# A decoder step on one core: index keys stored in operand layout, sample attention spread over the projections

## The chip, the cores and the metric

One core of a Trainium2 chip runs the whole layer. The engines are named as in the profile: PE (matmul; PEld its weight load), DVE (vector), ACT (scalar), POOL, and SP, which only issues DMAs here. The metric is the device time of one launch in microseconds (us). Three timed runs of the kernel before gave 902.44, 902.24 and 901.87 us, a median of 902.24.

## The reference

One layer for a prompt of 512 new tokens and for 8 sample sequences of 4 new tokens each with 2048 cached positions. The parts that matter here:

```python
hn = _rmsnorm(x, g_pre_mix)
xl, gate, q, k, v, qi, ki, wi = _split_proj(hn @ w_in)      # and rotary on q, k, qi, ki
lru, hT, new_buf = _rglru(xl, ...)                          # conv taps, block gates, linear recurrence
att = attend(q, k, v, qi, ki, wi)
mix = concat(lru * gelu(gate), att) @ w_out                 # then norm, residual, squared-ReLU MLP

# a sample sequence: keys of 16 cached pages + 4 new ones
ki_past = cache_kidx[page_table].reshape(DB, PAST_LEN, IDX_DIM)
sc = einsum(relu(einsum(qi, ki_all) * IDX_DIM**-0.5), wi) * IDX_HEADS**-0.5
_, idx = top_k(where(kpos <= qpos, sc, -inf), 256)
# softmax over the 256 chosen keys (gathered from cache_k and cache_v), 8 heads of 64
```

The prompt has the same indexer and attention among its own 512 positions, with 128 chosen keys. The kernel does not gather the chosen keys: it scores all of them and adds a mask of 0 or -2^100.

## The kernel before, in words

All activations are stored transposed, channels on partitions and the 544 tokens (512 + 32) on the free axis, in two halves of 272. Each engine has its own straight program; the order on an engine is the order in which the code is written, and semaphores with counts tie the engines together. PE's program is the spine:

1. The input norm, then the projections of the index queries (QI, 4 tiles of 128 channels), of index key and head weights (KW), and the first tile of Q. A tile is 2 halves of 8 matmuls (`product`, L1229, `tile_product`, L1239); POOL applies the rotary (`rope`, L436) to what ACT copies out of PSUM (`rotary_tile`, L538).
2. The prompt's indexer (L1280 to L1290): scores on PE, ReLU on ACT (L584), weighting on DVE (L977). DVE then picks the prompt's top 128 (L987 to L993) and after it the sample's top 256 (L1008 on), one after the other.
3. The sample's indexer (L1293 to L1330), in two groups `g` of four sequences. POOL gathers the cached index keys by page table, 16 keys of 64 numbers to a partition (`gather`, L423, four gathers to a group into `kidx_in_sb`). PE transposes them (L1304), ACT copies the result to `kidxT` (L591), PE multiplies with the index queries (L1318), ACT applies the ReLU (L601), and PE sums the heads (L1325). Tile 1 of Q stands between the groups, tiles 2 and 3 after them.
4. K, XL (recurrent branch), GATE and V projections (L1372 to L1387). After every tile `unit_end` (L1361) does two *key steps* (`key_scores`, L1335): a step is one page of keys of four sequences, four DMAs of 256 KB issued by SP (`stream`, L358) into one of three slots of `kv`. 32 steps make the sample's scores `S`. The first needs `qbd`, which ACT builds (L617) from the rotated Q. The same `unit_end` also carries the recurrence of the four channel tiles: taps on ACT (`lru_taps`), sums on POOL (L463), gates on PE and ACT (`lru_gate`, L1358; `lru_gates`, L642), decay, root, and a scan on DVE (L1006) that frees the buffers for the next tile.
5. Scores of the new keys (L1394); ten mask products (L1408), each followed by a DVE add and maximum on `S` (L1068); two exponentials of 128 x 2080 on ACT (L720).
6. The prompt's attention, 32 units of one head and one query block (L1481): scores L1451, masked maximum on DVE L1081, exponential on ACT L736, transposes L1463, values L1476. In the same loop stand the ten transposes of the sample's probabilities (L1421) and one *value step* to a unit (`value_products`, L1426): a page of values of four sequences, streamed by SP through five slots, three of `kv` and two in the weight ring `wring`.
7. The sample's result is scaled (L1108), transposed (L1498) and copied, and the output projection (L1517) and the MLP follow, as long as everything before.

Weights come in blocks of 2 MB in the two halves of `wring`, loaded by SP or ACT (`load_block`, L555) when the block before in that half has been used.

## Time and profile before

| what | value |
|---|---|
| timed runs | 901.87 to 902.44 us, median 902.24 |
| the profiled execution | 901.47 us, its span 899.6 us |
| PE busy | 821.6 us, 91% of the span |
| DVE, ACT, POOL busy | 389.3, 348.5, 149.5 us |
| sample's indexer (stage 3) | from 79.4 us to the next Q tile at 113.0 |
| first key step | 139.1 us |
| masks (stage 5) | from 306.6 us |
| prompt attention with the value steps | 312.6 to 410.5 us |
| output projection starts | 414.55 us |
| DMA traffic | 133.21 MB, 148 GB/s on average; 383 GB/s from 350 to 410.5 us |

Times of a row are from the start of the span; the profiled execution is 1.87 us longer than its span and 0.77 us under the median. In a timeline row stand start, duration, engine, line, operation, output and inputs, count of records, and in brackets how long the engine had been idle and what ended that. A matmul in 32-bit floats leaves two records, so a tile of 16 matmuls shows as x32.

### The profile page before, as it was taken

The numbers are of one execution on the slowest core, as the hardware profiler recorded it, in microseconds if no ns is written. First come the engines' busy times: TensorE is split into PE (matmuls) and PEld (weight loads), VectorE is DVE, ScalarE is ACT, GpSimd is POOL, SyncE is SP. The second block draws the span as 40 slices with busy tenths as digits, with TensorE's granted clock in tenths as the row PEclk, the third lists the DMA queues.
The fourth block names the chain that finished last, engine by engine and source line by source line (L and its number), as shares of the span: only waits on it lengthen the run. The fifth ranks groups of instructions, "written<-read, shape, count | busy, mean of one in ns | idle before, by whom it ended". The sixth has DMA issues, their size and how long they took to land.

```text
span 899.6 us, 16220 instructions
## 1 busy us (share of the span) xinstructions
PE 821.6 (91%) x6089; PEld 673.0 (75%) x6089; DVE 389.3 (43%) x780; ACT 348.5 (39%) x744; POOL 149.5 (17%) x153
## 2 busy tenths in 40 slices
PE   5987799989999897988997999999999999999990
PEld 3863477777765442335886899999999999999990
DVE  6219999994000342430178544332212433433327
ACT  3556465355555462431253434322222433322120
POOL 0631064433233500000000111100000111100000
PEclk9999999999999987997998999999999999999996
DMA  8420416777758869992011222222222222222202
GB/s 343 161 94 28 159 72 206 253 258 241 247 191 300 281 233 391 387 387 89 1 48 47 71 79 85 93 95 80 84 93 94 71 93 93 70 95 94 93 24 99
DMA packets 52180, 133.21 MB, mean 148 GB/s; under 512 B 6113, under 2 KB 6626, under 8 KB 50850
## 3 DMA queue, kind: packets, MB, share of 16 engines
q1 hardware_dynamic: 49442, 113.08, 36.3%
q10 hardware_dynamic: 864, 10.58, 3.3%
q0 software_dynamic: 1824, 8.86, 2.6%
q8 instruction: 33, 0.54, 0.2%
q14 instruction: 17, 0.14, 0.0%
HBM read 127.84 MB, written 4.67 MB: 147 GB/s over the span
## 4 chain that ended last, share of the span: by engine, by line
PE 74%; DVE 7%; DMA 6%; SPq 5%; ACT 4%; issue 3%; POOL 1%; DVEq 0%; ACTq 0%
PE bank L1529 42%; PE bank L1235 20%; SPq L365 4%; PE bank L1346 3%; PE bank L1384 3%; DMA arena<-in_ck 3%; DMA wring<-in_cv 2%; DVE scp L977 1%; PE bank L1358 1%; ACT lx L634 1%; PE bank L1318 1%; PE bank L1304 1%; DVE lx L913 1%; DMA arena<-in_cv 1%; PE bank L1434 1%
## 5 line engine op out<-in xcount | busy, mean ns | idle before, releaser
L1235 PE MATMUL bank<-regR,wring 128*128 128x272 f32 x640 | 152.8, 399 | 7.5 <-DVE regR L924 4.4
L1235 PEld LDWEIGHTS bank<-regR,wring 128*128 128x128 f32 x640 | 122.0, 192 | 35.3 <-issue 5.3
L1164 DVE TENSOR_TENSOR h_lo<-lx,h_hi 128x544 f32 (+1 forms) x32 | 35.9, 1121 | 111.0 <-ACT h_hi L827 110.7
L1529 PE MATMUL bank<-h_lo,w_hi_odd 128*128 128x272 f32 x256 | 73.9, 289 | 0.0
L1529 PE MATMUL bank<-h_hi,w_hi_even 128*128 128x272 f32 x256 | 73.8, 288 | 0.0
L1529 PE MATMUL bank<-h_lo,w_hi_even 128*128 128x272 f32 x256 | 73.7, 288 | 0.0
L1529 PE MATMUL bank<-h_hi,w_hi_odd 128*128 128x272 f32 x256 | 73.7, 288 | 0.0
L1529 PE MATMUL bank<-h_hi,w_lo_odd 128*128 128x272 f32 x256 | 73.6, 287 | 0.0
L1529 PE MATMUL bank<-h_hi,w_lo_even 128*128 128x272 f32 x256 | 73.5, 287 | 0.0
L506 POOL TENSOR_TENSOR lx<-lx 128x544 f32<-128x544 f32 x30 | 32.8, 1093 | 244.6 <-ACT lx L822 244.6
L1529 PE MATMUL bank<-hn_lo,w_hi_odd 128*128 128x272 f32 x240 | 69.3, 289 | 0.0
L1529 PE MATMUL bank<-hn_hi,w_hi_even 128*128 128x272 f32 x240 | 69.3, 289 | 0.0
L1529 PE MATMUL bank<-hn_lo,w_hi_even 128*128 128x272 f32 x240 | 69.1, 288 | 0.0
L1529 PE MATMUL bank<-hn_hi,w_hi_odd 128*128 128x272 f32 x240 | 69.1, 288 | 0.0
L1529 PE MATMUL bank<-hn_hi,w_lo_odd 128*128 128x272 f32 x240 | 69.0, 287 | 0.0
L1529 PE MATMUL bank<-hn_hi,w_lo_even 128*128 128x272 f32 x240 | 68.9, 287 | 0.0
L1116 DVE TENSOR_TENSOR w_lo_even<-wring,w_hi_even 128x1024 fp32r<-128x1024 f32 x32 | 39.2, 1225 | 66.4 <-ACT w_hi_even L788 66.4
L822 ACT ACTIVATE lx<-bank 128x272 f32<-128x272 f32 x60 | 23.9, 398 | 113.7 <-PE bank L1529 113.7
L1235 PE MATMUL bank<-regM,wring 128*128 128x272 f32 x256 | 60.8, 400 | 2.0 <-ACT regM L763 2.0
L1235 PEld LDWEIGHTS bank<-regM,wring 128*128 128x128 f32 x256 | 49.6, 194 | 12.8 <-ACT regM L763 2.4
L1116 DVE TENSOR_TENSOR w_lo_odd<-wring,w_hi_odd 128x1024 fp32r<-128x1024 f32 x32 | 39.0, 1220 | 44.2 <-ACT w_hi_odd L788 43.9
L788 ACT CAST w_hi_even<-wring 128x1024 fp32r<-128x1024 f32 x32 | 33.6, 1049 | 62.5 <-PE bank L1529 62.5
(259 smaller groups left out, 1683.7 us busy)
## 6 DMA issues: line engine op xcount, KB each, us to landing
arena<-in_ck SPq DMA_DIRECT2D x128, 256.0 KB, 3.9
wring<-in_w_mlp SPq DMA_DIRECT2D x64, 512.0 KB, 3.4
arena<-in_cv SPq DMA_DIRECT2D x80, 256.0 KB, 5.7
wring<-in_cv SPq DMA_DIRECT2D x48, 256.0 KB, 6.1
wring<-in_w_in ACTq DMA_DIRECT2D x4, 2048.0 KB, 8.5
wring<-in_w_in SPq DMA_DIRECT2D x2, 2048.0 KB, 13.1
regX<-in_xT SPq DMA_DIRECT2D x4, 544.0 KB, 5.5
regX<-in_xT POOLq DMA_DIRECT2D x1, 2176.0 KB, 11.3
```

Source lines behind the costliest of these rows:

```text
L365: eng.dma_start(slot[:, b4, :], table[bass.ds(page[b4], 1), :, :].rearrange("a p c -> p (a c)")).then_inc(landed, 16)
L506: nc.gpsimd.tensor_tensor(square_t[:, s, :], relu_t[:, s, :], relu_t[:, s, :], ALU.mult).then_inc(h_sq, 1)
L634: nc.scalar.activation(out[:, 0:SEQ], prompt, ACT.Identity, bias=bias, scale=w)
L788: nc.scalar.copy(w_hi[parity][:, :], w_raw[:, parity, :]).then_inc(w_hi_rd, 1)
L822: nc.scalar.activation(relu_t[:, parity, hf * HALF:(hf + 1) * HALF], bank[(2 * parity + hf) % 4][:, 0:HALF], ACT.Relu).then_inc(h_ev, 1)
L913: ins = vec.reciprocal(rstd[:, c], rstd[:, c])
L1116: vec.tensor_tensor(w_lo[parity][:, :], w_raw[:, parity, :], w_hi[parity][:, :].bitcast(F32), ALU.subtract).then_inc(w_lo_rd, 1)
L1164: vec.tensor_tensor(h_lo[:, at], square_t[:, parity, :], h_hi[:, at].bitcast(F32), ALU.subtract).then_inc(h_lo_rd, 1)
L1235: ins = pe.matmul(bank[e % 4][0:parts, 0:HALF], lhs(k), rhs[:, k, hf * HALF:(hf + 1) * HALF], start=(k == 0), stop=(k == KT - 1))
L1346: ins = pe.matmul(bank[4 + s % 2][32 * b4:32 * b4 + 32, 0:P], qbd[:, 4 * (s // NPG) + b4, m, :], kv[:, slot, b4, m * P:(m + 1) * P], start ...
L1384: ins = pe.matmul(bank[e % 4][0:n, :], hnT[:, k, j * P:j * P + n], w[:, k, :], start=(k == 0), stop=(k == KT - 1))
L1529: ins = pe.matmul(out, lhs[w][:, k * P:(k + 1) * P], rhs(k), start=(first and k == 0 and i == 0), stop=(last and k == KT - 1 and i == 2))
```

## The change

Four things are changed together, and the diff below is cut to them.

- **Index keys.** The host stores each page as 64 x 128 (channel by key), so PE needs no transposes. A page now lands in `kidxT[g]` directly. For group 0, SP issues 64 small DMAs (32 KB each, before the key stream); for group 1, POOL issues 32 gathers of 128 rows of 512 bytes instead of four of 128 rows of 4 KB, placed between its rotary tiles. ACT copies Q's first tile out between the two groups.
- **Key steps.** One stands in the middle and one at the end of each *half* tile of K and XL, so all 32 are done two projections earlier.
- **Sample attention.** New scores, masks, exponentials, transposes and the first 21 value steps move into GATE and V; the other eleven stand at every third unit of the prompt's attention. V's 32 sample rows are projected first (`V_ORDER`). DVE does scans 1 to 3 after the masks.
- **Slots.** Values use three slots instead of five; both halves of the output weight are loaded by ACT.

```diff
-V_SLOTS = 5
+V_SLOTS = 3
+V_ORDER = (4, 0, 1, 2, 3)
+MID_VALUES = 21
...
@@ SP @@
+            def index_keys(j):
+                eng.load(page_regs, steps[0:1, j * 4:(j + 1) * 4])
+                rows, cols = HD * (j // 8), P * (j % 8)
+                for b4 in range(4):
+                    page = eng.snap(page_regs[b4], min_val=0, max_val=NPOOL - 1)
+                    eng.dma_start(kidxT[0][rows:rows + HD, b4, cols:cols + P],
+                                  ci_d[bass.ds(page, 1), :, :].rearrange("a d k -> (a d) k")).then_inc(kidx_in[0], 16)
             eng.wait_ge(steps_in, 16)
+            for j in range(NPG):
+                index_keys(j)
             keys(0, 2, None, 0)
-            keys(1, 0, kx_tr, 16)
-            keys(2, 1, kx_tr, 16)
+            keys(1, 0, kd_mm, 5)
+            keys(2, 1, kd_mm, 5)
...
@@ POOL @@
+            def index_keys(first, last):
+                for n in range(first, last):
+                    b4, j = n // 8, n % 8
+                    gather(kidxT[1][:, b4, j * P:(j + 1) * P], ci_rows, row_i[:, b4, j:j + 1], kidx_in[1])
+            eng.wait_ge(hn_rd, 2 * KT)
+            index_keys(0, 4)
             for t in range(CT):
                 rope(t, qiT[:, t, :])
+                index_keys(4 + 2 * t, 6 + 2 * t)
             rope(4, kiT[0:HD, :], HD)
-            eng.wait_ge(kx_tr, 8)
-            for b in range(4):
-                gather(kidx_in_sb[:, b, :], ci_rows, row_i[:, 4 + b:5 + b], kidx_in)
+            index_keys(12, 32)
...
@@ ACT @@
             for g in range(GRP):
-                for u in range(8):
-                    eng.wait_ge(kx_tr, 8 * g + u + 1)
...
+                if g == 1:
+                    rotary_tile(5, E_Q)
                 for d in range(5):
...
             for m in range(CT):
-                rotary_tile(9 + m, E_K + 2 * m)
-                sample_scores(2 * m)
-                sample_scores(2 * m + 1)
+                rotary_tile(9 + m, E_K + 2 * m, scores=4 * m)
...
+            gate_out(0, 0)
+            gate_out(0, 1)
+            recurrence(4)
+            gate_out(1, 0)
+            sample_transposed(0)
...
+            gate_out(2, 1)
+            sample_exponentials(1)
+            recurrence(6)
...
@@ DVE @@
-            for c in range(CT):
-                scan(c)
+            scan(0)
             for g in range(GRP):
...
+            for c in range(1, CT):
+                scan(c)
...
@@ PE @@
+            w = weights(2)
+            for m in range(CT):
+                for hf in range(2):
+                    s = 4 * m + 2 * hf
+                    half_product(E_K, hf, m, lambda: key_scores(s))
+                    key_scores(s + 1)
...
+            w = weights(4)
+            half_product(E_GATE, 0, 0, new_key_scores)
+            masks(0, 1)
+            half_product(E_GATE, 1, 0, lambda: masks(2, 3))
+            masks(4)
+            recurrence_gates(1)
...
+            for i, j in enumerate(V_ORDER):
...
+                    if k in (2, 5):
+                        value_products(6 + 3 * i + k // 3)
...
-            for u in range(KSTEPS + 5):
+            for u in range(ATT_UNITS + 5):
                 if u < ATT_UNITS and u % 2 == 0:
                     att_scores(u // 2)
-                if u < 10:
-                    sample_transposes(u)
...
-                if u >= 5:
-                    value_products(u - 5)
+                if u % 3 == 1 and MID_VALUES + u // 3 < KSTEPS:
+                    value_products(MID_VALUES + u // 3)
```

What this does to the order on the engines, at three places. First PE from the end of the prompt's indexer to the first key steps. Before, L1304 are the transposes, L1318 the index products, L1235 projections and L1346 key steps:

```order
L1289 MATMUL bank<-arena,regQ 128x512 x8
L1304 MATMUL bank<-ident,arena 128x128 x32
L1318 MATMUL bank<-regX,arena 32x512 x16
L1318 MATMUL bank<-arena 32x32 x4
L1235 MATMUL bank<-regR,wring 128x272 x16
L1304 MATMUL bank<-ident,arena 128x128 x32
L1318 MATMUL bank<-regX,arena 32x512 x16
L1318 MATMUL bank<-arena 32x32 x4
L1325 MATMUL bank<-regM,wm 32x512 x8
L1329 MATMUL bank<-regM,wm 32x32 x2
L1235 MATMUL bank<-regR,wring 128x272 x48
L1346 MATMUL bank<-arena,qbd 32x128 x32
```

And now, where L1344 are the index products, L1270 projections and L1371 key steps:

```order
L1326 MATMUL bank<-arena,regQ 128x512 x8
L1344 MATMUL bank<-arena 32x512 x16
L1344 MATMUL bank<-arena 32x32 x4
L1270 MATMUL bank<-regR,wring 128x272 x16
L1344 MATMUL bank<-regX,arena 32x512 x16
L1344 MATMUL bank<-arena 32x32 x4
L1350 MATMUL bank<-regM,wm 32x512 x8
L1354 MATMUL bank<-regM,wm 32x32 x2
L1270 MATMUL bank<-regR,wring 128x272 x36
L1371 MATMUL bank<-arena,qbd 32x128 x16
L1270 MATMUL bank<-regR,wring 128x272 x4
```

The two groups of 32 transposes are gone, and the first key step stands 36 matmuls after the head sums instead of 48: after half of the first half tile of K, not after its first tile.

The second place is the end of GATE and the start of V on PE. Before, L1358 are the recurrence's gates and L1384 the V projection:

```order
L1235 MATMUL bank<-regR,wring 128x272 x16
L1358 MATMUL bank<-lx,wgate 128x272 x2
L1346 MATMUL bank<-arena,qbd 32x128 x32
L1358 MATMUL bank<-lx,wgate 128x272 x2
L1384 MATMUL bank<-wring,regR 128x512 x8
L1346 MATMUL bank<-arena,qbd 32x128 x32
```

Now L1448 are transposes of the sample's probabilities, L1462 value steps, L1385 gates and L1522 the V projection:

```order
L1270 MATMUL bank<-regR,wring 128x272 x4
L1448 MATMUL bank<-ident,regX 128x128 x4
L1462 MATMUL bank<-arena,regQ 32x512 x4
L1270 MATMUL bank<-regR,wring 128x272 x4
L1385 MATMUL bank<-lx,wgate 128x272 x2
L1462 MATMUL bank<-arena,regQ 32x512 x4
L1385 MATMUL bank<-lx,wgate 128x272 x2
L1522 MATMUL bank<-wring,regR 32x512 x3
L1448 MATMUL bank<-ident,regX 128x128 x4
L1462 MATMUL bank<-arena,regQ 32x512 x4
```

A value step of four matmuls stands between the two pairs of gates where two key steps stood, and the projections are cut in pieces of two to four matmuls.

The third place is POOL after the rotary of the index key. Before:

```order
L440 TENSOR_TENSOR lx<-lx 64x544
L441 TENSOR_TENSOR lx<-lx 64x544
L442 TENSOR_TENSOR arena<-lx 64x544
L425 DMA arena<-in_ci,row_i 128x1024 x4
L440 TENSOR_TENSOR lx<-lx 128x544
```

And now:

```order
L452 TENSOR_TENSOR lx<-lx 64x544
L453 TENSOR_TENSOR lx<-lx 64x544
L454 TENSOR_TENSOR arena<-lx 64x544
L430 DMA regX<-in_ci,row_i 128x128 x20
L452 TENSOR_TENSOR lx<-lx 128x544
```

Twenty gathers instead of four stand in POOL's queue ahead of the rotary of Q.

## Rows read from the trace of the kernel before

**Rows 1.** The page, part 4: shares of the chain by engine.

```profile
PE 74%; DVE 7%; DMA 6%; SPq 5%; ACT 4%; issue 3%; POOL 1%; DVEq 0%; ACTq 0%
```

**Rows 2.** Stretches: length, busy (count) of PE, PEld, DVE, ACT, POOL, PEclk, DMA, GB/s.

```profile
313.00:350.00 37.00, 31.23 (x196) 14.18 (x194) 12.59 (x72) 17.49 (x57) 2.13 (x5) 0.74 0.79 291
350.00:410.50 60.50, 53.33 (x418) 19.52 (x414) 21.70 (x80) 20.68 (x51) 0.00 (x0) 0.95 1.04 383
```

**Rows 3.** Timeline of PE, the sample's indexer to the first key step.

```profile
79.44 6.18 PE L1304 MATMUL bank<-ident,arena 128*128 128x128 f32 x32 [2.11 <-ACT arena L584]
86.30 3.71 PE L1318 MATMUL bank<-regX,arena 128*32 128x512 f32 x32 [0.68 <-ACT regX L591]
...
97.50 1.04 PE L1304 MATMUL bank<-ident,arena 128*128 128x128 f32 x8
...
103.26 3.71 PE L1318 MATMUL bank<-regX,arena 128*32 128x512 f32 x32 [0.68 <-ACT regX L591]
...
113.00 23.95 PE L1235 MATMUL bank<-regR,wring 128*128 128x272 f32 x96 [3.18 <-ACT lx L550]
139.11 1.95 PE L1346 MATMUL bank<-arena,qbd 128*32 128x128 f32 x64 [2.16 <-issue]
```

**Rows 4.** The gathers' line L425 on POOL, and POOL's idle time before them.

```profile
L425 POOL DMA_INDIRECT arena<-in_ci,row_i x8: 933/948/1170, 24.4 to 89.7; - x8
...
  issue: 1.8, 6
```

**Rows 5.** Timeline of POOL: end of the index key's rotary, and two of Q's.

```profile
58.73 1.32 POOL L442 TENSOR_TENSOR arena<-lx 64x544 f32<-64x544 f32 x1
...
114.98 1.34 POOL L440 TENSOR_TENSOR lx<-lx 128x544 f32<-128x544 f32 x1 [24.39 <-ACT lx L550]
...
131.67 2.28 POOL L440 TENSOR_TENSOR lx<-lx 128x544 f32<-128x544 f32 x1 [3.27 <-ACT lx L550]
```

**Rows 6.** Timeline of ACT: last copy of Q, building qbd, a table load.

```profile
130.05 1.54 ACT L550 COPY lx<-bank 32x272 f32<-32x272 f32 x4
137.20 1.81 ACT L617 COPY qbd<-regQ 64x32 f32<-64x32 f32 x8 [5.61 <-POOL regQ L442]
...
223.47 1.28 ACT L642 ACT_TABLE_LOAD   x1
```

**Rows 7.** Timeline of PE: two key steps, a tile, a stalled key step.

```profile
148.53 1.95 PE L1346 MATMUL bank<-arena,qbd 128*32 128x128 f32 x64
150.41 7.60 PE L1235 MATMUL bank<-regR,wring 128*128 128x272 f32 x32
...
182.47 1.93 PE L1346 MATMUL bank<-arena,qbd 128*32 128x128 f32 x32 [4.62 <-DMA arena<-in_ck]
```

**Rows 8.** Timeline of SP: the key stream, and later two steps and two more.

```profile
14.35 265.72 SPq L365 DMA_DIRECT2D arena<-in_ck  x120
280.89 4.42 SPq L365 DMA_DIRECT2D wring<-in_cv  x8
285.97 4.42 SPq L365 DMA_DIRECT2D arena<-in_ck  x8
```

**Rows 9.** DMA issues, keys and weights: count, KB each, us to landing.

```profile
arena<-in_ck SPq DMA_DIRECT2D x128, 256.0 KB, 3.9
...
wring<-in_w_in ACTq DMA_DIRECT2D x4, 2048.0 KB, 8.5
```

**Rows 10.** The chain of waits in the XL stage: start, us, what.

```profile
170.22 12.21 DMA arena<-in_ck
```

**Rows 11.** Timeline of PE: first masks, first scores of the prompt's attention.

```profile
306.57 0.49 PE L1408 MATMUL bank<-smask,ind_r 32*128 32x512 f32 x2 [0.18 <-ACT arena L708]
...
312.60 0.80 PE L1451 MATMUL bank<-arena,regQ 64*128 64x128 f32 x4
```

**Rows 12.** Timeline of DVE: the sample's mask is done; the last scaling.

```profile
211.24 0.44 DVE L1056 TENSOR_SCALAR smask<-arena 128x544 fp32r<-128x544 f32 x1
...
410.64 0.75 DVE L1108 TENSOR_SCALAR lx<-bank,sstat 128x512 f32<-128x512 f32 x1 [8.40 <-PE bank L1438]
```

More of the change, by code:

```diff
@@ L229, in build @@
         w_in = [sem("w_in_even"), sem("w_in_odd")]
-        kidx_in = sem("kidx_in")
+        kidx_in = [sem(f"kidx_in{g}") for g in range(GRP)]
         kv_in = [sem(f"kv_in{i}") for i in range(3)]
@@ L381, in _ @@
                     keys(i * 3 + (3 + j), (j + 2) % 3, k_mm, i * 3 + (j + 1))
-            for s in range(3, V_SLOTS):
-                values(s, s, gemm_mm, E_V)
             for s in (30, 31):
@@ L545, in rotary_tile @@
                 for hf in range(2):
+                    if scores is not None:
+                        sample_scores(scores + 2 * hf)
                     src = gemm_out(e + hf)
@@ L553, in rotary_tile @@
                     last.then_inc(gemm_ev, 1)
+                    if scores is not None:
+                        sample_scores(scores + 2 * hf + 1)
             def load_block(n):
@@ new lines, in _, with gate_out @@
+            for m in range(CT):
+                s = 16 + 4 * m
+                sample_scores(s)
+                recurrent_half(m, 0)
+                sample_scores(s + 1)
+                sample_scores(s + 2)
+                recurrent_half(m, 1)
+                if m == 1:
+                    recurrence(m, lambda: sample_scores(s + 3))
+                else:
+                    sample_scores(s + 3)
+                    recurrence(m)
+            load_block(5)
+            def gate_out(m, hf):
+                src = gemm_out(E_GATE + 2 * m + hf)
+                nc.scalar.activation(mixT[:, m, hf * HALF:(hf + 1) * HALF], src[:, 0:HALF], ACT.Gelu_apprx_tanh).then_inc(gemm_ev, 1)
@@ new lines, in _ @@
+            w = weights(2)
+            for m in range(CT):
+                for hf in range(2):
+                    s = 4 * m + 2 * hf
+                    half_product(E_K, hf, m, lambda: key_scores(s))
+                    key_scores(s + 1)
+            w = weights(3)
+            for m in range(CT):
+                for hf in range(2):
+                    s = 16 + 4 * m + 2 * hf
+                    half_product(E_XL, hf, m, lambda: key_scores(s))
+                    if m == 1 and hf == 1:
+                        lru_gate(0, 0)
+                        lru_gate(0, 1)
+                    key_scores(s + 1)
+                if m == 1:
+                    lru_gate(0, 2)
+                    lru_gate(0, 3)
@@ new lines, in new_key_scores @@
+            def new_key_scores():
+                eng.wait_ge(rope_out, 13)
+                eng.wait_ge(k_ev, KSTEPS)
+                for g in range(GRP):
+                    for m in range(CT):
+                        for b4 in range(4):
+                            ins = pe.matmul(bank[4 + g][32 * b4:32 * b4 + 32, 0:NS], qbd[:, 4 * g + b4, m, :], kT[:, m, SEQ:NT],
+                                            start=(m == 0), stop=(m == CT - 1))
+                    ins.then_inc(kn_mm, 1)
@@ new lines, in sample_mask @@
+            def sample_mask(n):
+                g, c = n // 5, n % 5
+                cols = slice(c * 512, min((c + 1) * 512, NKEY))
+                if n == 0:
+                    eng.wait_ge(smask_rd, 1)
+                    eng.wait_ge(kn_ev, GRP)
+                elif n >= 2:
+                    eng.wait_ge(sm_ev, n - 1)
+                rows = slice(NS * min(c, 3), NS * min(c, 3) + NS)
+                taken = smask[rows, 0:CHUNK] if c < 4 else smask[rows, CHUNK:ROW]
+                pe.matmul(bank[4 + n % 2][:, 0:cols.stop - cols.start], ind_r[rows, g, :], taken, start=True, stop=True).then_inc(sm_mm, 1)
@@ new lines, in _ @@
+            transposes_and_values(6, 3)
+            half_product(E_GATE, 1, 3, lambda: transposes_and_values(7, 4))
+            recurrence_gates(2, lambda: value_products(5))
+            w = weights(5)
+            for i, j in enumerate(V_ORDER):
+                n = P if j < 4 else NS
+                e = E_V + i
+                slot_free(e)
+                for k in range(KT):
+                    ins = pe.matmul(bank[e % 4][0:n, :], hnT[:, k, j * P:j * P + n], w[:, k, :], start=(k == 0), stop=(k == KT - 1))
+                    if k == 2 and i < 2:
+                        sample_transposes(8 + i)
+                    if k in (2, 5):
+                        value_products(6 + 3 * i + k // 3)
+                ins.then_inc(gemm_mm, 1)
+                if i == 2:
+                    recurrence_gates(3, lambda: value_products(8 + 3 * i))
+                else:
+                    value_products(8 + 3 * i)
```

268 lines of the change are left out of this document (121 added, 147 removed).

## The prediction

> **What bounds the kernel now.** I read the chain of waits first, then the stretches, then PE's timeline stage by stage. The chain is 74% PE [rows 1], so a microsecond is won only where PE does work that can go, or stands still. From the first key step to the output projection the reader is to look at PE's busy time together with its granted clock: in the attention, 313 to 410.5 us, PE is busy 31.23 us at a mean clock of 0.74 and 53.33 us at 0.95 [rows 2]. At the full 2.4 GHz that is about 31.23 x 0.74 + 53.33 x 0.95 = 73.8 us of work in 97.5 us, so 23.7 us are lost there, while the DMA engines are full (share 1.04, 383 GB/s, rows 2): the 32 value steps are all streamed in this stage. Two other losses stand in PE's timeline: the transposes of the index keys, and the mask products. The MLP behind is untouched.
>
> **Index stage.** The transposes take 86.30 - 79.44 = 6.9 us and 103.26 - 97.50 = 5.8 us of PE's time, ACT's copies between them included, and tile 2 of Q then waits 3.18 us for ACT, which has not yet copied tile 0 out [rows 3]. The change copies that tile between the groups. So Q's tile 2 starts at 113.0 - 12.7 - 3.2 = 97.1 us and tile 3, with 7.5 us a tile (rows 7: 7.60 for x32, with an overlap), ends at 112.2. Then the gain is partly given back: half a half tile later, at 114.1, PE reaches the first key step, which needs qbd. Behind tile 3's end lie five copies on ACT (1.9 us; four take 1.54, rows 6), one rotary of three POOL operations of 1.34 (4.0 us, rows 5; not the 2.28 of the last one before, when DVE was in a different operation), and ACT's 1.81 (rows 6). That makes 120.1 us: PE waits 6.0 us with the rest of K queued behind. Before, the first key step ran at 139.11 with a whole tile of K done (7.5 us), now with a quarter (1.9). Lead: 139.1 - 120.1 - 5.6 = 13.4 us. After a 3.18 us wait the next three tiles took 23.95 instead of 22.6 us [rows 3]; I take the same 1.4 us off for the half clock after this wait. **11.9 us.**
>
> This needs the index keys in time. Group 0: 64 issues on SP. Two steps of four DMAs with their register loads start 5.08 us apart [rows 8], so 16 steps take 41 us from 14.35 us on [rows 8] and are 20 us early for 79.4; what they hold up, the first key loads, is wanted only at 120. Group 1: a gather costs POOL 0.95 us and 0.3 of idle [rows 4]. The twelve early ones fit into gaps in which POOL waits for ACT; the last twenty run from 60.05, the end of the index key's rotary [rows 5], to 85.1, and the dots of group 1 start at 79.4 + 3.8 + 7.5 = 90.7. The cover is 5.6 us, less landing; behind the gathers the rotary of Q is queued, for which nobody waits before 87. If the pitch were 1.55 us, the cover would be gone.
>
> The rows show gathers issued every 1.25 us without waiting for one another [rows 4]. The Trainium skill, "DMA: Bandwidth & Descriptors", section "Anatomy of one DMA — SWDGE (gpsimd) path", puts about 2 us of fixed cost on each such DMA, and its rules for kernel authors call transfers below 64 KB mostly overhead. If that cost were paid one after another, the last twenty would end at about 100 instead of 85 us; that is the first rival below.
>
> **Key steps.** The interval between key steps falls from 4.7 us to (7.5/2 + 2 x 0.95)/2 = 2.83 us [rows 7]. A step is four DMAs of 256 KB [rows 9], 1.05 MB, which is 2.74 us at 383 GB/s [rows 2], and 2.54 us of SP's time [rows 8]. Both are just below 2.83. From the release of a slot to its next use there are 3 x 2.83 - 0.95 = 7.5 us; the fourth DMA is issued 1.5 us after the release and lands 3.9 us later [rows 9], 5.4 us. So the K stage keeps up with 97% of the DMA rate; I take 1.5 us of jitter (0 to 14: half a microsecond on 28 steps). XL has the GATE weights (2048 KB, rows 9) and the stores of K (as much as half of that and a little) on top, 2.1 and 1.2 MB: 3.3 MB are 8.6 us at 383 GB/s, less 2.1 us of slack. Before, the same transfers made one step land after 12.21 us [rows 10] and PE wait 4.62 us [rows 7]. Net **-2 us** (1 to -8).
>
> The same page of the Trainium skill, section "Specifications", gives about 358 GB/s of HBM to a core, by which a step would take 2.93 us and the 29 streamed steps some 3 us more than I sum. The trace does not agree: 383 GB/s over 60 us [rows 2].
>
> **GATE and V.** Here PE only gets work that it did later: ten masks, ten transposes, 21 value steps. That shift is worth nothing by itself. What it removes: from the first mask to the first attention scores PE needed 6.0 us [rows 11] for ten products of some 0.25 us (0.49 for two): **+3.5 us**, the adds on DVE being hidden under GATE's products. The mask itself is ready at 211.2 [rows 12], by a chain on DVE that starts with the prompt's indexer and is not shortened; PE wants it at about 222 (120 + 43 of K + 54 of XL + 5), so it is not late. What it adds: ACT's gates need a table load of 1.28 us [rows 6], which two key steps (1.95 us) covered; now one step or none stands there. Some 0.9 us on each of four: **-3.5 us** (0 to -10; the two exponentials and eight copies also stand in ACT's queue between GATE's evictions). V runs three value steps in 7 + 3 us per tile, 3.4 us each, slower than the stream; the output weight's 2.1 MB in between costs **-1.5 us** (0 to -5).
>
> **Attention.** Eleven value steps instead of 32, 11.5 MB with 5.4 MB of x, V and weights, are 44 us of DMA in some 53 us, so the stream should no longer bound it. Bounds for the loss: 0, and the 23.7 us of today. I take 8, a third, for the start of the pipeline, the small first blocks where DVE and ACT set the pace, and the burst of other transfers: **+15.7 us** (0 to 23.7). At the end the first of the two scalings, 0.75 us [rows 12], is no longer hidden: **-0.8**.
>
> **Sum.** 11.9 - 1.5 - 2 + 3.5 - 3.5 - 1.5 + 15.7 - 0.8 = 21.8 us, from the profiled 901.47 to 879.7. The runs shown have their median 0.77 higher, so I say **880 us**.
>
> **Rivals.**
> - *Index keys late.* If the gathers cost 2 us each, the last lands near 102 us and PE waits 11 us at group 1: 891. For it: these gathers are eight times as many, and DVE is busy in the prompt's indexer meanwhile. Against: same 128 rows, same 0.95 us while DVE was picking [rows 4].
> - *The stream or PE's queue takes back more.* Half a microsecond per key step (14 us), or an attention that keeps most of its loss because DVE and ACT set its pace: 890 to 898. For it: 97% use with three slots, PE's program in order. Against: 3.9 us of landing in 7.5.
> - *Slower than before: the slot turn bounds the keys.* If under load every key step landed like the one of rows 10, a step would take (1.5 + 12.2 + 0.95)/3 = 4.9 us, 28 steps 57 us more, 937 us. It decides against the change from 21.8/28 = 0.78 us more per step on, a landing of 8.4 us. For it: one such landing is seen. Against: it shared the engines with two other transfers, and the stream of values held 383 GB/s [rows 2].
> - *Better.* Jitter, table loads and burst all hidden: 866 to 870.
> - *The work only moves*, and gives no time: within 0.2% (1.8 us, about what a measurement can tell).
>
> **How the numbers follow.** Forecast, 870 to 889: 0.52. Index keys late: 0.10. More taken back: 0.17. Better: 0.08. No change: 0.03. Slower: 0.10. Faster is 0.52 + 0.10 + 0.17 + 0.08 = 0.87, same 0.03, slower 0.10. The range 866 to 897 holds the forecast, the first two rivals nearly and most of the better case, some 0.8.
>
> **What would show it.** Right: no transposes between 79 and 97 us and the last head sum near 97; the first key step near 120 after a wait of about 6 us for ACT's qbd; key steps 2.8 us apart in K with waits on DMA only in XL; no stage of its own for the masks; an attention of 50 to 60 us with a clock near 1.0; the output projection starting near 393. Wrong: a wait for the index keys at 91 us, waits on DMA before most key steps in K, or an attention still over 75 us.

## The result, and the profile after

The changed kernel took **897.84 us** in the median (896.25 to 901.7, 11 runs) beside 903.44 us of the kernel before (901.87 to 907.61, 11 runs) on the same chip: a ratio of 0.9945, 95% interval 0.9929 to 0.9961. It is faster by 0.55% (5.6 us between the medians); 22 us were forecast. The time lies 0.84 us above the top of the range.

The profiled execution took 901.08 us (span 899.3), one of the slowest of the eleven. A second profile of the same kernel (e16 below, 898.61 us) is read beside it. Most of the miss lies between the first key step and the output projection, and there the two agree: 290.9 and 289.7 us.

The chain of waits, page part 4, shares of the span by engine and by line [rows 1]:

```profile
PE 84%; DVE 6%; DMA 4%; ACT 3%; issue 1%; POOL 0%; SPq 0%; ACTq 0%; DVEq 0%
PE bank L1617 42%; PE bank L1270 23%; PE bank L1522 4%; PE bank L1371 3%; PE bank L1462 3%; DMA arena<-in_cv 2%; DMA arena<-in_ck 1%; PE bank L1541 1%; PE bank L1553 1%; PE bank L1566 1%; PE bank L1256 1%; PE bank L1344 1%; DVE scp L1012 1%; DVE lx L948 1%; PE bank L1673 1%
```

PE holds 84% of it in place of 74%: the waits for others became PE's own work. The index stage, PE's timeline (start, us, line, tiles, count, idle before) [rows 3]:

```profile
82.25 3.82 PE L1344 MATMUL bank<-arena 128*32 128x512 f32 x40 [2.11 <-ACT arena L598]
86.00 7.60 PE L1270 MATMUL bank<-regR,wring 128*128 128x272 f32 x32
93.53 3.71 PE L1344 MATMUL bank<-regX,arena 128*32 128x512 f32 x32
...
98.04 1.92 PE L1350 MATMUL bank<-regM,wm 128*32 128x512 f32 x16 [0.68 <-ACT regM L610]
...
122.99 1.93 PE L1371 MATMUL bank<-arena,qbd 128*32 128x128 f32 x32 [6.20 <-issue]
```

The transposes are gone, the second group of index keys is not waited for at 93.53, and the first key step waits 6.20 us for qbd, as forecast (6.0). It stands at 123.0 and not at 120.1 because this execution ran its first 50 us at a mean clock of 0.93; in e16 the clock there was 1.00 and the step stood at 120.38. The last gather, POOL's timeline [rows 4]:

```profile
84.10 1.47 POOL L430 DMA_INDIRECT regX<-in_ci,row_i  x1 [0.30 <-issue]
...
88.38 0.94 POOL L430 DMA_INDIRECT regX<-in_ci,row_i  x1 [0.30 <-issue]
```

Key steps of K, and the stall in XL, PE's timeline [rows 7]:

```profile
131.63 1.08 PE L1371 MATMUL bank<-arena,qbd 128*32 128x128 f32 x32
132.64 2.10 PE L1270 MATMUL bank<-regR,wring 128*128 128x272 f32 x8
134.67 1.08 PE L1371 MATMUL bank<-arena,qbd 128*32 128x128 f32 x32
...
187.37 1.94 PE L1371 MATMUL bank<-arena,qbd 128*32 128x128 f32 x32 [7.00 <-DMA arena<-in_ck]
189.23 3.99 PE L1270 MATMUL bank<-regR,wring 128*128 128x272 f32 x8
```

The interval of two key steps is 134.67 - 131.63 = 3.04 us with no wait for data, where 2.83 was forecast. The start of the attention, PE, then DVE, then POOL:

```profile
340.54 0.49 PE L1541 MATMUL bank<-arena,regQ 64*128 64x128 f32 x4
346.27 1.08 PE L1553 MATMUL bank<-ident,arena 128*128 128x128 f32 x2 [5.24 <-DVE arena L1123]
...
350.79 1.93 PE L1462 MATMUL bank<-arena 128*32 128x512 f32 x8 [1.68 <-DMA arena<-in_cv]
...
359.62 1.93 PE L1462 MATMUL bank<-arena 128*32 128x512 f32 x8 [4.33 <-DMA arena<-in_cv]
```

```profile
340.85 5.36 DVE L1123 TENSOR_SCALAR arena<-arena,stat 128x128 f32<-128x128 f32 x1
346.53 0.29 DVE L1123 TENSOR_SCALAR arena<-arena,stat 128x128 f32<-128x128 f32 x1
```

```profile
340.53 1.35 POOL L502 TENSOR_TENSOR regM<-regM,arena 128x544 f32<-128x544 f32 x1
...
344.99 1.13 POOL L502 TENSOR_TENSOR regM<-regM,arena 128x544 f32<-128x544 f32 x1
```

The first normalisation on DVE takes 5.36 us, the next one 0.29, and it ends at 346.21 us, as POOL's four gate multiplications do (346.12). The stretches (columns as in [rows 2]): the K stage, then the attention.

```profile
139.00:172.00 33.00, 33.00 (x440) 24.47 (x439) 31.54 (x64) 13.13 (x38) 9.96 (x8) 1.00 1.00 344
...
339.00:347.00 8.00, 2.63 (x22) 1.07 (x18) 6.79 (x13) 2.54 (x8) 7.58 (x15) 0.77 0.98 343
347.00:372.00 25.00, 18.98 (x87) 7.10 (x91) 8.34 (x48) 7.77 (x32) 0.80 (x2) 0.53 0.88 335
372.00:410.00 38.00, 35.65 (x300) 17.64 (x292) 23.49 (x90) 22.18 (x59) 0.00 (x0) 1.00 0.38 123
```

Here the reader is to see two things. In K the DMA engines are full (share 1.00) at 344 GB/s, not at the 383 of the value stream before [rows 2]. And of 71 us of attention 2.63 x 0.77 + 18.98 x 0.53 + 35.65 = 47.7 us are work at 2.4 GHz: 23.3 us are lost, as many as before (23.7).

**Where the 17 us went.** PE's busy time times its granted clock, summed over slices of 1 us, is its work; the rest of the time is lost. K and XL count from the first key step to GATE's first product; the middle column runs on to the first scores of the attention, masks included; the attention ends at the transposes of the sample's result.

| length, work, lost | K, XL | GATE, V, masks | attention |
|---|---|---|---|
| before | 76.3, 70.0, 6.3 | 97.2, 90.9, 6.3 | 97.9, 74.0, 23.9 |
| after, e16 | 110.8, 97.0, 13.7 | 106.2, 103.4, 2.8 | 68.7, 48.7, 20.0 |

Over the three stages the work grew by 249.1 - 234.9 = 14.2 us, and the loss is 36.5 us in both. The sum of the prediction has 5.6 us more work here (three quarters of a K tile, now behind the first key step) and 8.5 us less loss (15.7 in the attention, 3.5 of masks, less 1.4, 1.5, 2, 3.5, 1.5 and 0.8). So **8.6 us are work that the sum did not have, and 8.5 us are losses that did not go**; together 17.1 us, the miss.

The work can be placed. In K and XL before has 70.0 us, to which the change adds the 5.6 and eight pairs of key steps of 1.9 us that stood in GATE and V: 90.8 us, where e16 has 97.0. That is 6.2 us more; the other two columns together have the other 2.4.

### The profile page after: what moved, and what is told of

It reads as the page before. It is cut to its first block, busy times and chain, and to the rows that moved or that the text cites. A ratio compares the mean times of both kernels' runs of the same rounds, so it can differ in the third digit from the quotient of the medians.

```text
span 899.3 us, 16317 instructions
## 1 busy us (share of the span) xinstructions
PE 824.6 (92%) x6025; PEld 664.1 (74%) x6025; DVE 387.2 (43%) x780; ACT 341.4 (38%) x730; POOL 173.9 (19%) x177
## 4 chain that ended last, share of the span: by engine, by line
PE 84%; DVE 6%; DMA 4%; ACT 3%; issue 1%; POOL 0%; SPq 0%; ACTq 0%; DVEq 0%
PE bank L1617 42%; PE bank L1270 23%; PE bank L1522 4%; PE bank L1371 3%; PE bank L1462 3%; DMA arena<-in_cv 2%; DMA arena<-in_ck 1%; PE bank L1541 1%; PE bank L1553 1%; PE bank L1566 1%; PE bank L1256 1%; PE bank L1344 1%; DVE scp L1012 1%; DVE lx L948 1%; PE bank L1673 1%
## 5 line engine op out<-in xcount | busy, mean ns | idle before, releaser
L1270 PE MATMUL bank<-regR,wring 128*128 128x272 f32 x640 | 166.2, 412 | 3.2 <-DVE regR L959 3.2
L1270 PEld LDWEIGHTS bank<-regR,wring 128*128 128x128 f32 x640 | 121.8, 196 | 38.8 <-issue 14.4
L857 ACT ACTIVATE lx<-bank 128x272 f32<-128x272 f32 x60 | 23.9, 398 | 113.7 <-PE bank L1617 113.7
L1270 PE MATMUL bank<-regM,wring 128*128 128x272 f32 x256 | 60.9, 401 | 2.3 <-ACT regM L798 2.3
L1270 PEld LDWEIGHTS bank<-regM,wring 128*128 128x128 f32 x256 | 49.6, 194 | 13.1 <-ACT regM L798 2.5
```

Of the source, the lines that this page charges most:

```text
L857: nc.scalar.activation(relu_t[:, parity, hf * HALF:(hf + 1) * HALF], bank[(2 * parity + hf) % 4][:, 0:HALF], ACT.Relu).then_inc(h_ev, 1)
L1270: ins = pe.matmul(bank[e % 4][0:parts, 0:HALF], lhs(k), rhs[:, k, hf * HALF:(hf + 1) * HALF], start=(k == 0), stop=(k == KT - 1))
```

## The experiments

Times are medians; ratios are to the kernel before, run beside on the same chip. Lengths are from PE's timelines, us: K and XL from the first key step to the first products with the new keys, then GATE and V, then the attention up to the output projection.

| run | us | ratio (95%) | first key step | K, XL | GATE, V | attention |
|---|---|---|---|---|---|---|
| after | 897.84 | 0.9945 (0.9929 to 0.9961) | 123.0 | 112.0 | 104.1 | 74.8 |
| e16 after again | 899.01 | 0.9945 (0.9924 to 0.9966) | 120.4 | 112.8 | 104.2 | 72.8 |
| e1 pairs | 900.79 | 0.997 (0.9955 to 0.9984) | 122.9 | 112.1 | 104.3 | 72.9 |
| e2 POOL first | 898.26 | 0.9948 (0.9929 to 0.9966) | 121.0 | 112.2 | 104.1 | 72.7 |
| e3 late reload, stores | 891.77 | 0.9868 (0.9841 to 0.9894) | 123.0 | 112.3 | 104.3 | 65.3 |
| e5 four slots | 896.08 | 0.992 (0.9895 to 0.9945) | 120.4 | 107.9 | 104.1 | 74.0 |
| e6 four slots, pairs | 893.68 | 0.99 (0.9878 to 0.9921) | 122.5 | 104.7 | 104.5 | 74.0 |
| e7 GATE weights later | 898.78 | 0.995 (0.9931 to 0.9968) | 121.6 | 110.4 | 104.5 | 74.1 |
| e8 = e6, e2, e3 | 884.93 | 0.9805 (0.9782 to 0.9828) | 120.7 | 105.0 | 104.6 | 66.4 |
| e10 first tile whole | 882.53 | 0.9764 (0.9744 to 0.9783) | 120.3 | 101.4 | 104.3 | 68.5 |
| e12 and GATE weights | 879.63 | 0.9742 (0.9719 to 0.9764) | 121.5 | 99.2 | 104.5 | 65.5 |
| e13 output block late | 891.91 | 0.9875 (0.986 to 0.9891) | 122.7 | 109.4 | 104.3 | 65.7 |
| e14 x late alone | 893.82 | 0.9893 (0.9877 to 0.9909) | 122.7 | 112.7 | 104.1 | 68.2 |
| e15 all late | 876.19 | 0.9704 (0.9686 to 0.9721) | 121.1 | 102.6 | 104.6 | 58.7 |

Three more have the order of the kernel before: e4 (896.75 us, 0.9924, 0.9903 to 0.9945), e11 (899.1 us, 0.9944, 0.9925 to 0.9962), e9 (916.44 us, 1.0169, 1.0139 to 1.02).

**e1, key steps in pairs.**

```diff
-                    half_product(E_K, hf, m, lambda: key_scores(s))
+                    half_product(E_K, hf, m, None)
+                    key_scores(s)
                     key_scores(s + 1)
```

> The two key steps of a half product of K and XL both stand behind it, so that no half of these 16 is cut in the middle; ACT's copies follow that order; all else is the changed kernel. Price-of-a-cut theory: before, a tile of K with one cut and two key steps took 9.42 us; after, with four cuts and four key steps, 12.16, so a cut costs (12.16 - 4 x 0.945 - 7.53)/3 = 0.28 us. Two cuts per tile go, on 8 tiles 16 x 0.28 = 4.5 us: about 893.3 us (ratio to the kernel before 0.9895), a tile of K at 11.6 us. Rival, each key step pays for its own wait wherever it stands: no change, 898 us (0.994), a tile still at 12.1. Rival, two key steps in a row run ahead of the stream: a wait on DMA in front of the second one, 898 us or more.

No faster than the change (0.997 beside 0.9945). The profile of e1 (PE) has the saving and what became of it:

```profile
151.12 1.08 PE L1370 MATMUL bank<-arena,qbd 128*32 128x128 f32 x32 [0.27 <-DMA arena<-in_ck]
152.13 3.94 PE L1269 MATMUL bank<-regR,wring 128*128 128x272 f32 x16
156.00 1.08 PE L1370 MATMUL bank<-arena,qbd 128*32 128x128 f32 x32
157.31 1.08 PE L1370 MATMUL bank<-arena,qbd 128*32 128x128 f32 x32 [0.23 <-DMA arena<-in_ck]
```

A whole half takes 156.00 - 152.13 = 3.87 us where two pieces took 2 x 2.03, but in K a wait for data of 0.23 to 1.50 us now stands before the second key step of five of the eight pairs: the stream cannot follow. The price of a cut is real and was hidden by the slots. The first theory had no such limit; the third expectation came true.

**e2, POOL's multiplications first.**

```diff
-            eng.wait_ge(gemm_ev, E_WO)
-            eng.dma_start(v_d[0:SEQ, :].rearrange("(j p) c -> p j c", p=P), v[:, 0:4, :]).then_inc(state_stored, 16)
-            eng.dma_start(v_d[SEQ:NT, :], v[0:NS, 4, :]).then_inc(state_stored, 16)
+            eng.wait_ge(gemm_ev, E_GATE + 2 * CT)
             for c in range(CT):
...
             eng.dma_start(lru_d, pack[:, :, :]).then_inc(state_stored, 16)
+            eng.wait_ge(gemm_ev, E_WO)
+            eng.dma_start(v_d[0:SEQ, :].rearrange("(j p) c -> p j c", p=P), v[:, 0:4, :]).then_inc(state_stored, 16)
+            eng.dma_start(v_d[SEQ:NT, :], v[0:NS, 4, :]).then_inc(state_stored, 16)
```

> POOL's four gate multiplications (with their small copies) stand ahead of the stores of V, so that they run right behind the last scan at some 333 to 339 us and are over when the attention's first normalisation on DVE comes; all else is the changed kernel. Theory that DVE's first normalisation of 5.36 us (0.29 for the others) is long because POOL multiplies at the same time: it takes 0.3 us, PE's wait of 5.24 us before the first transpose goes, 4 to 5 us faster, about 893.5 us (0.9895). Rival, the stream decides there: PE goes to its value step 22 sooner and waits that much longer for the data, which land when they land; 897 us (0.993).

DVE's first normalisation, and PE's next wait:

```profile
339.11 0.35 DVE L1124 TENSOR_SCALAR arena<-arena,stat 128x128 f32<-128x128 f32 x1
```

```profile
349.17 1.93 PE L1463 MATMUL bank<-arena 128*32 128x512 f32 x8 [7.73 <-DMA arena<-in_cv]
```

0.35 us in place of 5.36: the two engines did collide. But the time stays, since PE waits 7.73 us for value step 22 in place of 1.68. The rival had it right.

**e3, the reload of x and the stores of V behind value step 27.** The stores are taken from their place ahead of the multiplications.

```diff
             eng.wait_ge(st_tr, 10)
+            eng.wait_ge(v_mm, 28)
+            eng.dma_start(v_d[0:SEQ, :].rearrange("(j p) c -> p j c", p=P), v[:, 0:4, :]).then_inc(state_stored, 16)
+            eng.dma_start(v_d[SEQ:NT, :], v[0:NS, 4, :]).then_inc(state_stored, 16)
             eng.dma_start(regX[:, :], xT_d).then_inc(x_again, 16)
```

> The reload of x (2.2 MB) and the stores of V (1.1 MB) are issued behind value step 27 and not at the start of the attention; all else is the changed kernel. Theory that this burst keeps value steps 22 and 23 from landing: their waits of 1.68 and 4.33 us go, and with them the half clock up to 372 us; 6 us of waits, less what stays behind DVE's slow normalisation, and up to 3 us of clock: about 891 us (0.987; 888 to 895). Rival, the output weight's block (2.1 MB) or the three slots hold the stream anyway: 896 us (0.992). Rival, the late reload now stands in the way at the attention's end or of the residual: 900 us or more.

In time as the first theory has it: 0.9868 beside the change's 0.9945, some 7 us of 903. The attention is 7.4 to 9.4 us shorter in the profile than in the two of the change. The wait before step 23 is gone, but not the one before step 22:

```profile
348.58 1.93 PE L1463 MATMUL bank<-arena 128*32 128x512 f32 x8 [2.84 <-DMA arena<-in_cv]
```

POOL's multiplications still met DVE there, one at a time, and PE's wait for DVE falls to 0.89, 1.03 and 0.61 us in place of 5.24. So more than the two transfers changed here; e14, which keeps the 5.24, is the cleaner test:

```profile
341.25 1.01 DVE L1124 TENSOR_SCALAR arena<-arena,stat 128x128 f32<-128x128 f32 x1
342.58 1.04 DVE L1124 TENSOR_SCALAR arena<-arena,stat 128x128 f32<-128x128 f32 x1
```

**e4 and e11, the index keys' part alone, and with x's reload late.** The edit of e4 is the index part of the diff on the kernel before; e11 adds the wait for v_mm 28 ahead of the reload.

> The kernel before with the index keys' part of the change alone (layout, SP's and POOL's loads, no transposes, tile 0 of Q copied between the groups); the attention of the sample stands where it stood before. In the changed kernel this part brought the first key step from 139.1 to 123.0 us with a quarter tile of K done in place of a whole one: 10.5 us of lead. Theory that this lead is worth itself: 893 us (0.9885). Then the other part of the change, the spreading, loses 5 us net. Rival, the lead is lost at the attention, where the stream of values sets the pace but does not start earlier: no, since it starts with V's end, which moves too; still, if the mask of the top-k chain or the stream binds, 898 to 903 us (0.994 to 1.0), and the spreading gains 0 to 5 us.

> The index keys' part alone as in e4, and x's reload (2.2 MB) behind value step 27; the attention of the sample stands where it stood before. Theory that the late reload is worth as much without the spreading, since there the stream of values bounds the attention and gets rid of 2.2 MB at 386 GB/s, 5.6 us: 891 us (0.986). Then the spreading in itself gains nothing (e3 has 891.8). Rival, without the spreading the values do not come faster, or the reload now stands before the residual: 896 us (0.992).

The index part alone is as fast as the whole change (0.9924 and 0.9945, overlapping intervals), so the spreading as it stands gains nothing that was measured. The first key step of e4 is 17.3 us earlier, the first scores only 7.0 (305.59 in place of 312.60). PE's waits in e4:

```profile
167.29 1.93 PE L1339 MATMUL bank<-arena,qbd 128*32 128x128 f32 x32 [6.77 <-DMA arena<-in_ck]
...
215.85 2.18 PE L1351 MATMUL bank<-lx,wgate 128*128 128x272 f32 x4 [7.84 <-POOL lx L475]
```

The second is for a recurrence whose scan stands behind the mask's selection on DVE, which the change does not shorten:

```profile
206.31 0.44 DVE L1061 TENSOR_SCALAR smask<-arena 128x544 fp32r<-128x544 f32 x1
206.67 1.28 DVE L1011 TENSOR_TENSOR_SCAN arena<-lx 128x544 f32<-128x544 f32 x1
```

e11 misses its first theory: without the spreading the late reload gains nothing (the last values wait up to 6.90 us), with it x's reload alone gains some 5 us (e14). That fits a spreading that makes room, which the burst had filled; a reload later than step 28 was not tried without the spreading.

**e5 and e6, a fourth key slot, without and with pairs.**

```diff
+        k_slot = [kv[:, 2], kv[:, 0], kv[:, 1], regM[:, 0:2048].rearrange("p (b c) -> p b c", b=4)]
...
-            with eng.Fori(0, 9) as i:
-                for j in range(3):
-                    keys(i * 3 + (3 + j), (j + 2) % 3, k_mm, i * 3 + (j + 1))
+            with eng.Fori(0, 7) as i:
+                for j in range(4):
+                    keys(i * 4 + (4 + j), j, k_mm, i * 4 + (j + 1))
```

> A fourth slot for the key steps, in the part of regM that is free until GATE's first eviction; values keep their three slots; all else is the changed kernel. In K the DMA engines were full (share 1.00) at 344 GB/s, below the 383 on which the prediction rests. Slot theory: three slots keep too few transfers in flight; with four the stall of 7.00 us in XL behind the GATE weights shrinks by one more step of cover, 3.0 us, or more if the rate rises, and with it the half clock behind it: 893.5 us (0.990). Rival, the engines carry no more than 344 GB/s of key steps beside this work: the stall only shifts a step, 897 us (0.9935) or at best 3 us less stall that comes back as waits later in XL.

> Four key slots as in the run before, and both key steps of a half behind it (no cut in the middle), K and XL alone. e1 showed what hid the price of a cut: PE's half with two key steps took 5.74 us without a wait in place of 6.08, and the saved time came back as waits for key loads. Slot theory: no waits in K, a tile at 2 x 5.74 = 11.5 us in place of 12.16, 8 x 0.66 = 5.3 us, with the 3 to 4 us of the stall 889 us (0.985). Rival, the engines are full at 344 GB/s: 3.05 us a key step whatever PE does, waits on DMA before the second step of most pairs, 898 to 901 us (0.994 to 0.997) as in e1.

K and XL shrink by 4.1 and 7.4 us in the profiles; in time e6 gains 0.45% on the change (0.99 beside 0.9945), e5's interval overlaps the change's. With four slots the pairs hardly wait in K: its tiles take 11.49 us (e8: 131.07 to 142.56), as the price of a cut says. The same stretch moves 349 GB/s in e6 and, with the same code of K, 358 in e8:

```profile
139.00:172.00 33.00, 32.77 (x473) 26.22 (x472) 31.55 (x64) 12.57 (x38) 13.20 (x11) 1.00 1.01 358
```

Both are beyond the 344 of three slots. But a stall of 5.8 us stays in XL, so the rival is right there. e6's work from the first key step to the first scores of the attention is 194.2 us, 6.1 less than after's 200.3 with 16 cuts less: 0.38 us a cut.

**e7, the GATE weights later.** The call that loads them stands behind XL's second tile on ACT.

> ACT issues the load of the GATE weights (2 MB) behind the second tile of XL (about 222 us in place of 172 us); all else is the changed kernel. Theory that the stall of 7.00 us in XL is this load beside the stores of K: the stall at 187 shrinks to what the stores (1.2 MB) cost, 1 to 2 us; the load then competes with the last key steps, and GATE, which needs the weights at some 225, starts 5 to 8 us late or not at all: 893 to 898 us (0.989 to 0.994). Rival, the stores and not the weights make the stall: it stays at 5 us or more, and the time is 897 us or worse.

Nothing (0.995 beside 0.9945). The stall parts into 1.52 us at 186.78 and 3.79 us at 214.24 and goes with the transfer: with three slots the bytes are paid wherever they are put. (With four slots and a whole first tile, e12 against e10, the profile's K and XL are 2.2 us shorter.)

**e8, four edits at once: e6, e2 and e3.**

> Four key slots, the key steps in pairs, POOL's gate multiplications ahead of the attention, and x's reload and V's stores behind value step 27. Slot theory: 6 us of e3, 1 of DVE's start that is no longer hidden behind the stream, and 8 of e6: 883 us (0.977). Rival, engines full at 344 GB/s in K and XL: only the 6 to 8 us of the attention, 889 to 891 us (0.986).

884.93 us lies between the two, nearer the first. PE still waits for value step 22:

```profile
340.37 1.93 PE L1465 MATMUL bank<-arena 128*32 128x512 f32 x8 [5.92 <-DMA arena<-in_cv]
```

**e9, the kernel before with three value slots.**

```diff
-V_SLOTS = 5
+V_SLOTS = 3
...
-            with eng.Fori(0, 5) as i:
+            with eng.Fori(0, 9) as i:
```

> The kernel before with three slots for the value steps in place of five; nothing of the change. It measures the rate on which the prediction built (386 GB/s from 351 to 410 us, with five slots) as the changed kernel has it, with three. Slot theory: the values come at some 344 GB/s as the keys did with three slots, 3.05 us a step in place of 2.72, and the two steps that were loaded beside V's products come in the attention: (32 x 3.05 + 0) - (32 - 2) x 2.72 = 16 us longer, 919 us (1.018). Rival, the rate belongs to the stage and not to the slots: 386 GB/s, only the two steps later, 5 us, 908 us (1.006).

The slot theory, within 3 us. The stretch that gave the prediction its rate [rows 2]:

```profile
351.00:410.00 59.00, 47.11 (x384) 18.82 (x380) 22.27 (x85) 22.26 (x56) 0.00 (x0) 1.00 0.99 345
```

345 GB/s in place of 383 on the same stage and the same transfers, PE waiting up to 1.6 us before every second or third step in most of the stretch. The rate belongs to the slots.

**e10 and e12, K's first tile before its key steps; and the GATE weights behind XL's first tile.**

```diff
+                if m == 0:
+                    tile_product(E_K, w, 0, hnT)
+                    for s in range(4):
+                        key_scores(s)
+                    continue
```

> As e8, and K's first tile is computed whole before the first four key steps, which then stand in a row, so that the tile covers the wait for qbd (6.2 us in the changed kernel, 4.4 in e8). Theory that this wait and the half clock behind it (its first pieces took 1.93 and 3.81 us in place of 1.01 and 2.03) cost PE's time: 4.4 + 2.7 us, 878 us (0.9725). Rival, the stream decides when XL ends, and it starts no sooner, since the first slot comes free when qbd is there, at some 121 us, in both: 884 us (0.980), the gain comes back as a longer stall in XL.

> As e10, and ACT issues the load of the GATE weights behind the first tile of XL in place of before it, away from the stores of K. Theory that the stall in XL is one burst of 3.3 MB that two smaller ones avoid, with four slots as cover: 3 to 4 us less than e10, 875 us (0.969). Rival, engines full: the same time as e10, waits in other places.

e10 (0.9764 beside e8's 0.9805) lands between its two theories: the wait at the first key step is 0.72 us, but a new one of 2.32 us for ACT's copies, one of 0.77 us for keys in K and 3.55 and 1.44 us in XL take a part back. e12 shows no measurable gain over e10 (the intervals overlap).

**e13, e14 and e15: which transfer holds the values.** e13 issues the output weight's first block behind unit 16 of the attention, e14 x's reload alone behind value step 27, e15 all three late on top of e12.

```diff
             for u in range(ATT_UNITS + 2):
...
+                if u == 16:
+                    load_block(6)
```

> ACT issues the load of the output weight's first block (2 MB) in the middle of the attention, behind its unit 16, in place of V's end; all else is the changed kernel. Theory that this block holds value steps 22 and 23: their waits of 1.68 and 4.33 us go, though DVE's 5.24 stays: 893.5 us (0.9895). Rival, the two transfers of POOL's queue hold them: 897.5 us (0.994), the waits stay above 4 us in sum. Rival, each of the three has its share by bytes (2.1 of 5.4 MB): 2.3 us, 895.5 us (0.992).

> x's reload alone is issued behind value step 27; V's stores and the output weight's block stay at the attention's start; all else is the changed kernel. Theory that each of the three has its share by bytes (2.2 of 5.4 MB): 2.5 us of the 6, 895.5 us (0.992). Rival, the reload is what held the stream in e3 (it alone reads, as the values do): 892 us (0.987). Rival, it comes late anyway (issued at 347, the waits end at 351 and 360): only the wait of 4.33 us before step 23 goes, 894 us (0.990).

> As e12, and the output weight's first block issued in the middle of the attention as in e13. Theory that the last of the three transfers holds the values there: the wait of 5.88 us before value step 22 goes, and the half clock behind it: 872 to 874 us (0.967). Rival, the slots decide (three for the values, V's products and value steps having used them up): the wait stays at 3 us or more, 878 us (0.972).

> The changed kernel once more. Expected 898 us (0.9945, 0.993 to 0.996), from the first key step to GATE's first new key scores 112.0 us, from there to the first attention scores 104.1, from there to the output projection 73 to 75 us; the first key step at 120.3 or at 123.0 us, as the clock of the first 50 us was 1.00 or 0.93.

e13: both waits for values are gone, DVE's 5.24 us stay, and 13.4 us are lost in the stage; part of its profile's gain (K and XL at 109.4) is a shorter XL stall, which its edit does not touch. e14: the wait of 4.33 us is gone, 2.26 us stand before step 22: the third expectation, and not a share by bytes. So the waits come of all three in the same 20 us, and **taking either the block or x away gives most of the gain** (6.3 and 4.7 us) that e3 had with x and the stores (7). What is left shows when DVE no longer covers it: with x and the stores late and DVE free, step 22 is held for 5.92 us in e8 and 5.88 in e12, and e15, which differs from e12 by the block alone, has no such wait. V's stores alone were not tried, nor more value slots beside the burst. Only e15 has neither DVE's wait nor one for values before 371 us, at full clock:

```profile
328.23:383.33 55.10, 49.58 (x405) 23.66 (x401) 33.86 (x148) 32.40 (x97) 2.61 (x4) 1.00 0.78 285
```

There 5.5 us are lost, where the change loses 20.0 to 23.2 and the prediction took 8. e15 is the fastest version: 876.19 us, 3.0% below the kernel before. It lies between its two expectations: the wait is gone, but its profile's K and XL are 3.4 us longer than e12's, with the same code. e16 repeats its expectation.

## Why the prediction was wrong

1. **Index stage: right.** +11.9 us; the first key step at 120.38 us in e16, 120.1 forecast (its own terms add up to 119.9); the wait for qbd 6.2 for 6.0. The index keys are in time on both queues, with 4.2 us of cover before landing where 5.6 were summed: the last twenty gathers take 27.1 us in place of 25.1 (62.18 to 89.32). The Trainium skill's 2 us for each gather ("DMA: Bandwidth & Descriptors", section "Anatomy of one DMA — SWDGE (gpsimd) path"), paid one after another, would by an estimate have made PE wait at 93.53 until 102 (62.18 + 20 x 2): it did not.
2. **Key steps: the interval was wrong.** "(7.5/2 + 2 x 0.95)/2 = 2.83" takes a product cut in four as dear as a whole one. A tile of one piece takes 7.53 us, of two 2 x 3.87, of four 4 x 2.03: 0.2 us at each start; two key steps in a row 1.88, two apart 2 x 1.01: 0.14. A cut costs some 0.33 us. K and XL have some 24 more starts of a product and 16 more of a key step, about 7 us by these prices, near the 6.2 of work found there; the sum had no term for it. "That shift is worth nothing by itself", said of GATE and V, is likely the same error: their products are cut too, and there and in the attention the work is 2.4 us more. No run takes the cuts of GATE and V out by themselves.
3. **The stream's rate was taken from another set-up.** "97% of the DMA rate" rests on 383 GB/s with five slots; with three it is 345 (e9). Here it stayed just enough for the slowed-down interval (1.05 MB in 3.04 us are 345 GB/s), so it cost little by itself, but it is why removing cuts won nothing until a fourth slot came (e1, e6).
4. **K and XL's losses: half right.** One stall in XL, 7.0 us (7.9 in e16) where 8.6 less 2.1 = 6.5 were forecast, and none in K. Missing was most of the half clock: behind the stall (1.94 + 3.99 us for what takes 1.01 + 2.03) and behind the wait for qbd (2.7 us in e16, 1.4 forecast). The two projections lose 7.4 us more than before, 4.9 forecast (1.4, 1.5 and 2).
5. **GATE and V: better than forecast**, at 104.1 to 104.6 us in every run; masks at no stage of their own, as forecast. The 3.5 us set aside for ACT's gates were four waits of 0.4 to 1.0 us, one of them in XL, and the 1.5 for the stream did not come: the stages lose 3.5 us less than before, where the sum had 1.5 more (3.5 + 1.5 - 3.5).
6. **Attention: the term that failed most.** The sum has "+15.7 us", less 0.8 at the end; 23.9 - 20.0 = 3.9 us came in e16 and 0.7 in the first profile. That is 11 us too few in e16, of which GATE and V made up 5. The bounds held (0 to 23.7), the value taken did not. "The stream should no longer bound it" counted 44 us of DMA against 53 us of stage as if spread evenly; the 5.4 MB of other transfers are issued from 338 to 347 us and take the DMA engines together with the value steps for the first 20 us. PE waits there, and its granted clock is 0.53 in the mean up to 372 us, near the lower of its two levels (1.2 of 2.4 GHz). With all three transfers late and DVE free the stage loses 5.5 us (e15), so the room was there. The collision of POOL and DVE was not in the sum at all; it cost nothing by itself (e2).

The rival "the stream or PE's queue takes back more" (890 to 898), given 0.17, has the time, and its mechanism in part. A key step did cost more in PE's program, 0.21 us and not half a microsecond, for the cuts; the attention did keep most of its loss, but for the burst of transfers and not "because DVE and ACT set its pace".

## What to carry to other kernels

A stream's rate is read from a stage with the same number of slots, or it is not read at all. Work that is spread between pieces of a product pays at every cut; count the cuts, and ask whether the stream hides or shows the price. Where a bound is removed from a stage, list everything that is issued at its start and when its first consumer needs it: here a reload for the residual, far behind, and a weight block took what the change had won.

## What the runs showed that was not expected

- A tensor_scalar of DVE between SBUF tiles took 5.36 us beside a row of four POOL multiplications, 1.01 to 1.04 us when it met them one at a time, and 0.29 to 0.35 without them. The Trainium skill ("SBUF — State Buffer", section "Who interferes with whom") says that DVE in a two-port mode, which a tensor_scalar can enter, and GpSimd (POOL here) share a pair of ports, and that the one that issues second blocks until the other's instruction is over. By that rule the wait would end with the multiplication under way. e3 agrees: there it ends 0.08 us behind it, three times. In the changed kernel it lasts over all four. Why the two differ is open.
- The DMA share reads 0.99 to 1.01 at 344 GB/s (three slots) and 349 and 358 (four), and 1.04 at 383 (five, [rows 2]). In a slice of the changed kernel's attention, with the burst's transfers beside the values, it reads 1.06 at 443: a full share is no sign that the rate can't rise.

```profile
350.98:356.92 5.94, 4.32 (x19) 1.36 (x13) 1.42 (x9) 1.55 (x7) 0.00 (x0) 0.50 1.06 443
```

- The limit of the Trainium skill that the prediction set aside ("DMA: Bandwidth & Descriptors", section "Specifications", about 358 GB/s of HBM for a core) lies between the 345 of three slots and the 383 of five, and would have been the nearer one for the keys. The kernel before ran above it, at 383, for 60 us.
- Left open: the stall in XL was 7.0 to 8.2 us in five profiles with the same code up to there, and 2.9 and 1.4 us in e13; in e15 it is 2.6 and 3.8 us, in e12, the same code up to there, 2.7 and 1.2. And the clock of the first 50 us was 0.93 or 1.00 in profiles of the same kernel, which moves all that follows by some 2.5 us.
